# Where expert matrices are held and how the expert loop is cut, in a two-layer decoder step on one core

## What is computed

```python
scores = sigmoid(x @ w_router)                      # 16 experts, top 2 of the best group
combine = sum(one_hot(idx, 16) * w[..., None], 1)
h = silu(einsum('td,edf->tef', x, wg)) * einsum('td,edf->tef', x, wu)
h = h * combine[..., None]
out = einsum('tef,efd->td', h, wd)                  # then a layer norm
```

## Time and profile before

| | us |
|---|---|
| median of 3 runs | 1433.53 |
| lowest and highest | 1431.14 and 1434.43 |
| profiled execution, its own time | 1433.79 |
| its span in the trace | 1432.2 |
| PE busy with matmuls | 1220.3 (85%) |
| DVE, ACT, POOL busy | 463.7, 259.4, 155.9 |
| HBM read | 341.47 MB |

### The profile page before, as it was taken

One profiled execution on the slowest core, in us unless ns is written; L12 is line 12 of the kernel. 1 busy time (PEld: TensorE's weight loads), 2 busy tenths in 40 slices (PEclk: granted clock), 3 DMA queues, 4 the chain that ended last, 5 costly groups with the idle time before them and its releaser, 6 DMA issues.

```text
span 1432.2 us, 26802 instructions
## 1 busy us (share of the span) xinstructions
PE 1220.3 (85%) x10864; PEld 789.4 (55%) x10865; DVE 463.7 (32%) x1207; ACT 259.4 (18%) x540; POOL 155.9 (11%) x249
## 2 busy tenths in 40 slices
PE   6998788999989989868996997999897799858950
PEld 4686555667747745434453776767575355434420
DVE  0025637312422423312334005133315134313235
ACT  0005622211411301100102112023204111101101
POOL 2005991000000000000002000000000000000022
PEclk9999988999999989978998896999997799989885
DMA  9656789733684689999958131235747797999420
GB/s 330 221 147 207 225 269 386 260 117 118 236 323 174 238 360 392 430 424 429 413 202 291 66 125 56 69 111 190 281 173 287 290 369 305 430 424 426 167 78 35
DMA packets 89237, 360.64 MB, mean 252 GB/s; under 512 B 7111, under 2 KB 7127, under 8 KB 72762
## 3 DMA queue, kind: packets, MB, share of 16 engines
q1 hardware_dynamic: 80418, 331.50, 60.6%
q0 software_dynamic: 8592, 27.68, 5.6%
q10 hardware_dynamic: 144, 0.26, 0.1%
HBM read 341.47 MB, written 18.38 MB: 251 GB/s over the span
## 4 chain that ended last, share of the span: by engine, by line
PE 71%; DMA 11%; DVE 10%; issue 4%; ACT 2%; SPq 1%; POOL 0%; POOLq 0%; DVEq 0%; ACTq 0%
PE acc L710 42%; PE psS L710 14%; DMA ring<-in_w_exp_up 8%; PE psV L710 6%; DVE mixq L1433 2%; PE acc L1002 2%; PE acc L813 1%; PE psN L1106 1%; DMA ring<-in_w_in_even 1%; PE acc L1136 1%; DMA arena<-by_slot,arena 1%; DVE arena L1816 1%; PE psN L710 1%; DVE arena L1818 1%; DMA by_slot<-zT 1%
## 5 line engine op out<-in xcount | busy, mean ns | idle before, releaser
L710 PE MATMUL acc<-xT,ring 128*128 128x288 f32 x768 | 192.8, 415 | 4.1 <-DMA ring<-in_w_in_even 4.1
L710 PE MATMUL psS<-ring,zT 128*32 128x256 f32 x2368 | 150.4, 411 | 30.0 <-DMA ring<-in_w_exp_up 24.2
L710 PEld LDWEIGHTS acc<-xT,ring 128*128 128x128 f32 x768 | 149.1, 195 | 47.2 <-issue 5.3
L710 PEld LDWEIGHTS psS<-ring,zT 128*32 128x32 f32 x2368 | 78.0, 118 | 101.5 <-issue 36.2
L710 PE MATMUL acc<-mixq,ring 128*128 128x288 f32 x512 | 127.7, 413 | 2.7 <-DVE mixq L1666 1.6
L1791 DVE COPY zT<-psV 32x256 f32<-32x256 f32 x208 | 87.0, 418 | 115.0 <-DMA by_slot<-zT 79.3
L710 PEld LDWEIGHTS acc<-mixq,ring 128*128 128x128 f32 x512 | 98.7, 193 | 31.1 <-DVE mixq L1666 2.0
L710 PE MATMUL acc<-arena,zT 128*32 128x256 f32 (+1 forms) x1296 | 98.0, 411 | 11.9 <-issue 8.4
L1308 ACT ACTIVATE arena<-acc 128x1024 f32<-128x1024 f32 (+7 forms) x98 | 72.1, 758 | 109.9 <-PE acc L710 34.5
L1782 DVE TENSOR_TENSOR zT<-zT,psS 64x256 f32<-64x256 f32 x52 | 22.1, 424 | 211.9 <-ACT zT L2047 211.9
L2166 POOL DMA_DIRECT2D by_slot<-zT x52 | 25.6, 492 | 546.8 <-DVE zT L1791 546.8
(11 more groups left out here) (331 smaller groups left out, 1369.0 us busy)
## 6 DMA issues: line engine op xcount, KB each, us to landing
ring<-in_w_exp_gate SPq DMA_DIRECT2D x22, 2048.0 KB, 14.0
ring<-in_w_exp_up SPq DMA_DIRECT2D x22, 2048.0 KB, 18.5
ring<-in_w_exp_down SPq DMA_DIRECT2D x22, 2048.0 KB, 18.1
mixq<-in_w_exp_down SPq DMA_DIRECT2D x10, 2048.0 KB, 11.2
arena<-in_w_exp_gate SPq DMA_DIRECT2D x10, 2048.0 KB, 12.6
arena<-in_w_exp_up SPq DMA_DIRECT2D x10, 2048.0 KB, 17.3
ring<-in_cache_k SPq DMA_DIRECT2D x64, 256.0 KB, 3.1
ring<-in_cache_v SPq DMA_DIRECT2D x64, 256.0 KB, 3.0
```

What stands on the lines that cost most here:

```text
L710: return pe.matmul(out, lhsT, rhs, start=first, stop=last)
```

## The change

Eleven places instead of nine can hold expert matrices. xT, rs and std now lie in one buffer with mixq and zT; a place WIDE covers the rest of qT, xT, rs and std, and is free once x has been transposed (`xtok`, tile 5). A place ARENA_D covers 2 MiB of the arena in the odd layer only. The even layer fills ten places in its first pass and the odd layer eleven; after that both cycle through nine, so from expert 4 on the wait is still for expert e - 3 (`matrix_done(..., NE * l + 2 + 3 * i + j // 3)`).

PE writes expert 0 out and runs experts 1 to 15 in a loop of five rounds of three. The last round skips the work for a following expert by `pe.If(i < last)`. `turn_h` moves from the end of one expert to behind the register loads of the next. At the head the order is fetch(0), turn_x(0), gate_and_up(0), fetch(1), turn_x(1), then the tile of memory keys (even layer), then expert 0. DVE's `pick(2)` moves behind `hidden(0)`. ACT follows the same order. YS moves to partitions 32 to 63 of the arena. GAMMA and BETA are loaded after POOL's loop, behind the last store.

```diff
-SLOTS, EXTRA = 6, 3
+SLOTS, EXTRA, CYCLE = 6, 5, 9
...
-        YS = work[0:CAP, 896:1920]
+        YS = arena[32:32 + CAP, 2048:3072]
...
-        extra = [mixq.rearrange("p f m -> p (f m)")[:, 0:UNIT], view(3072, UNIT), view(3072 + UNIT, UNIT)]
+        extra = [acts[:, 0:UNIT], view(3072, UNIT), view(3072 + UNIT, UNIT), acts[:, UNIT:2 * UNIT],
+                 view(12800, UNIT)]
...
             if k[2] == 0:
-                around = [(at + j) % SLOTS for j in range(SLOTS)]
-                cycle = around[:5] + [SLOTS + j for j in range(EXTRA)] + around[5:]
-                at = around[3]
-            PLACE.append(cycle[k[2] % len(cycle)])
+                turn = [turn[(at + j) % SLOTS] for j in range(SLOTS)]
+                if k[1] + 1 < DEPTH:
+                    first = turn[:5] + [MIXQ, ARENA_B, ARENA_C, WIDE] + turn[5:]
+                else:
+                    first = turn + [MIXQ, ARENA_D, ARENA_B, ARENA_C, WIDE]
+            n = k[2]
+            while n >= len(first):
+                n -= CYCLE
+            PLACE.append(first[n])
...
-                            matrix_done(sp, j % 3, NE * l + j // 3 - 2 + 3 * i)
-                        e = 3 * i + j // 3
+                            e, at = 4 + 3 * i + j // 3, u + 12 + j
+                            matrix_done(sp, j % 3, NE * l + 2 + 3 * i + j // 3)
...
-                if l + 1 < DEPTH:
-                    memory_keys(l + 1, (1,))
-
                 for i in range(6):
                     evacuated(pe, f"xtok{l}", i)
...
                     extra = pe.value_load(STEPI[0:1, bass.ds(2 * n, 1)], min_val=0, max_val=NFURTHER)
                     first = pe.value_load(STEPI[0:1, bass.ds(2 * n + 1, 1)], min_val=0, max_val=NCHUNK - 1)
+                    turn_h(S, first)
                     expert_in(e, 2, i)
...
+                    if last is None:
+                        on()
                     else:
+                        with pe.If(i < last):
+                            on()
                         pe.wait_ge(S.rows, c + 2)
                     down(S, c, Wd)
                     mark(to_mark, down_used)
-                    if into is not None:
-                        turn_h(S, c + 1)
...
                 turn_x(S, 0, to_turn)
-                fetch(S, 1, to_split, True)
                 expert_in(0, 0, 0), expert_in(0, 1, 0)
                 gate_and_up(S, 0, Wg, Wu)
+                fetch(S, 1, to_split, True)
                 turn_x(S, 1, to_turn)
-                turn_h(S, 0)
+                if l + 1 < DEPTH:
+                    memory_keys(l + 1, (1,))
                 pe.wait_ge(steps_ready, l + 1)
-                with pe.Fori(0, NE // 3 - 1) as i:
-                    expert(0, 3 * i, i, i)
-                    expert(1, 3 * i + 1, i, i)
-                    expert(2, 3 * i + 2, i, i + 1)
-                for e in range(NE - 4, NE):
-                    expert(e, e, e // 3, (e + 1) // 3 if e + 1 < NE else None)
+                expert(0, 0, 0)
+                with pe.Fori(0, NE // 3) as i:
+                    expert(1, 3 * i + 1, i)
+                    expert(2, 3 * i + 2, i)
+                    expert(3, 3 * i + 3, i, NE // 3 - 1)
...
-                if l + 1 == DEPTH:
-                    pool.dma_start(GAMMA, ln_g[l, 2:3].to_broadcast([P, D])).then_inc(ln_rows, 16)
-                    pool.dma_start(BETA, ln_b[l, 2:3].to_broadcast([P, D])).then_inc(ln_rows, 16)
...
                     pool.dma_start(by_slot[slot_rows(c)], YS).then_inc(S.stored, 16)
+                if l + 1 == DEPTH:
+                    pool.wait_ge(gate_up_used, NE * l + 1)
+                    pool.dma_start(GAMMA, ln_g[l, 2:3].to_broadcast([P, D])).then_inc(ln_rows, 16)
+                    pool.dma_start(BETA, ln_b[l, 2:3].to_broadcast([P, D])).then_inc(ln_rows, 16)
                 pool.wait_ge(S.stored, 16 * last + 16)
```

83 lines of the change are left out of this document (45 added, 38 removed).

## The result

The changed kernel takes 1413.24 us (median of 4 executions, 1408.51 to 1416.25), the kernel before beside it 1432.34 (4 executions): a ratio of 0.9871, interval 0.9828 to 0.9915. Forecast were 1426.3 us in a range of 1416 to 1438, so the direction held and the size did not. Two later comparisons on other chips gave 0.9897 (0.9814 to 0.9980) and 0.9929 (0.9905 to 0.9954). The first comparison was a favourable draw; 12 us is what there is to explain, 7 were forecast.

The account below looks back on a forecast made before the run. PE's path to expert 4's or 5's mark, a fixed weight stream, and PE's path from expert 12's matrices set each stage; -8.5 - 1.9 - 2.4 + 2.5 + 2.3 + 0.8 = -7.2 us gave 1426.3 us, range 1416 to 1438.

Parts of the forecast that it names:

- odd head: Odd layer's first experts: earlier first mark, but new code waits at experts 0, 1 and 3; +2.5 us, bounds -3 and +7.
- odd tail: Odd layer's expert 13: idle time by issue goes, fetch and gate and up at full speed; -8.5 us, between -7 and -9.5.
- even head: Even layer's start: first mark +2.6 us later, less slow clock at experts 0 and 1; -2.4 us, bounds +2 and -4.2.
- even tail: Even layer's last experts: idle times of 1.06 and 1.10 us go; -1.9 us, -1 to -2.2.
- register work: turn_h's wait from a loaded register at 21 experts, loop's If in five: +2.3 us, bounds 0 and 3.5.
- end: Kernel's end: GAMMA and BETA loads ahead of the six gathers in POOL's queue; +0.8 us, bounds 0 and 3.
- three written-out experts shorter (about 1565): Code up to the odd head, setting packet boundaries 76, 60 and 30 instructions behind jumps of experts 0, 1 and 3.
- price list: Odd head: jump to packet 3.7 or 6.3 us, less 2.3, 1.9, 0.9 before the boundary: waits 1.0, 3.1, 4.7 us.
- signs of being wrong: First-round waits of 6 us each, q8 packets in rounds 2 to 5, or no wait at expert 12's matrices.
- my bound of the rival: First-round jumps each wait 6.2 us, then run slow by 3.3: +17.5 at worst, +7.5 likelier, 1434; chance 0.20.
- The places: More matrix places cost at nothing, bounds 0 to -5 us a layer; rival that they help, 1421, chance 0.10.
- third part's stream: Stages' weight loads from expert 4 on: not moved by more places, each load still waiting for the same mark; 0 us.

Follow-up runs that it names:

- before_pad_28: Kernel before with 28 one-column matmuls (112 instructions) in front of the odd layer's router, nothing else changed: 1410.66 us; repeated as 28b, 1411.37 us.
- before_2: Kernel before, unchanged, run once more for a second trace: 1428.29 us, ratio 1.0007.
- pad_odd_17: Changed kernel with 17 one-column matmuls (68 instructions) in front of the odd layer's router: 1422.07 us, ratio 0.9950.
- old_head: Changed kernel with the old head order on PE and ACT (memory keys ahead of gathers, fetch(1) ahead of gate and up): 1406.09 us; repeated as old_head_2, 1408.30 us.
- loop_alone: Kernel before with only the recut loop (expert 0 written out, five rounds of three); nine places, old head order, old turn_h: 1414.75 us.
- pad_odd_27: Changed kernel with 27 one-column matmuls (108 instructions) before the odd layer's router, loop ending at 1813: 1433.95 us (1416.2 to 1463.5).
- pad_odd_54: Changed kernel with 54 one-column matmuls (216 instructions) before the odd layer's router: 1411.80 us, ratio 0.9884.
- old_head_pad_54: Changed kernel with the old head order and 54 one-column matmuls before the odd layer's router, none in the even layer: 1404.21 us, ratio 0.9833.
- pad_odd_21: Changed kernel with 21 one-column matmuls (84 instructions) before the odd layer's router, loop ending at 1789: 1422.88 us (1416.7 to 1429.8).
- pad_odd_23: Changed kernel with 23 one-column matmuls (92 instructions) before the odd layer's router, loop ending at 1797: 1434.71 us (1417.2 to 1447.7).

## Why the prediction was right or wrong

Each step beside what the traces give: two of the kernel before (four for the even layer, whose code before_pad_28 shares), three of the changed kernel.

| step | forecast, us | measured, us |
|---|---|---|
| odd head, to expert 4's first mark | +2.5 | -4.1 (102.2 to 98.1) |
| odd stream, expert 4 to 12 | 0 | +0.7 |
| odd tail, expert 12 to 15 | -8.5 | -8.4 (64.8 to 56.5) |
| even head, to expert 4's first mark | -2.4 | +0.1 (96.5 to 96.6) |
| even stream, expert 4 to 12 | 0 | -0.7 |
| even tail | -1.9 | -1.3 |
| register work, spread over the above | +2.3 | none of its own visible |
| end, behind expert 15's first mark | +0.8 | +0.9 (55.4 to 56.3) |
| sum | -7.2 | -12.8 |

The sum of -12.8 stands beside the 12.4 us of the three comparisons. The first comparison alone had 18.4; the rest of it lies outside these stages, and the 3.5 us between them are chance, as before_2 shows.

**The step that failed: the odd head.** It is 6.6 us off, more than the 5.6 us by which the sum is off. The mechanism held: a wait is the time from jump to packet less what PE does before the boundary. pad_odd_17, which puts the boundaries where I had them, came out 3.7 us above the kernel before at expert 4's mark (105.9 against 102.2) for a forecast of 2.5, and at 7.7 for 7.2 in time. What was wrong is the number under it, "three written-out experts shorter (about 1565)", by 185 instructions: 76, 60 and 30 should have been 147, 129 and 96. In its place the runs showed waits of 0, 2.15 and 2.61 us for the 1.0, 3.1 and 4.7 forecast, and a head of -4.1 us for +2.5.

The price list itself was only about right, and its working doesn't come out. From 3.7 us (expert 0) and 6.3 us (experts 1 and 3) to the packet, less 2.3, 1.9 and 0.9, the waits would be 1.4, 4.4 and 5.4 us, and the odd head +4.9 and not +2.5. pad_odd_17 has 0.71, 3.71 and 3.95. None of the signs of being wrong that I had named came: the first-round waits stayed far below 6 us, q8 was empty, and the waits at expert 12's matrices were there. No sign tested the count of places, which was the step that failed.

My range doesn't follow from my bounds either. They add up to 21.7 us below and 14.7 above the forecast, and two thirds of that are 14.5 and 9.8, so 1412 to 1436: not the -16 and +6 that I wrote, and not 1416 to 1438.

**The odd tail** was right in size (-8.4 for -8.5), and half right in cause. I read the 5.80 us as the price of code behind the loop. before_pad_28b keeps that code, its packets too, and loses 5.4 us of them, though 1.92 come back 62 matmuls on; its tail is 6.7 us shorter in all. What the kernel before paid was mostly a jump 17 instructions behind a boundary. Nor was my bound of the rival, that every first-round jump waits 6.2 us, near: the changed kernel's waits are 2.15 and 2.61.

**The even head** is 2.5 us worse than forecast, and by chance looked better in the first pair of traces. The 3.24 us of idle time are as forecast, and the first mark came at 503.40 for 505.7 forecast (1.3 us of this because the stage began sooner). But the 503.05 of the earlier trace rows to which I compared was a slow draw, 32.5 us behind the router: the four traces that share this code have 32.5, 30.2, 32.5 and 30.3. Old order with the rest of the change has it at 28.3. The order costs 6.3 us there, and I had valued its return, the 3.3 and 1.7 us of slow clock, as its own gain. I don't know which other part of the change gives that return: old_head differs from loop_alone (28.3 against 29.8 us, and 9.3 against 11.9 for expert 0) in the places, in `turn_h`'s place behind the register loads and in `pick(2)`, and these were not tried one by one.

**Register work**, +2.3 in the forecast, has no trace of its own in any stage, and 0.1 us in each of 26 places would have been 2.6. After the odd head it is the largest part of the miss towards faster.

**The places** were not worth nothing: 3 to 4 us in the even layer, 5.6 to 6.4 us in time. The false sentence is that the third part's stream begins at expert 4 in the even layer. I showed that it has no gap from there and took this for its beginning. In the kernel before, the DMA engines bring 388 GB/s from 503 to 569 us, with fortieths of this window at 139 to 238; in the changed kernel they bring 418 GB/s from 503 to 655 us, and after the first fortieth of this window no fortieth falls below 390. That is 29 matrices without a gap from expert 0's first mark. The bound that I gave, one matrix or 4.96 us, was nearer than my value. In the odd layer, where experts 1 to 5 hold PE longer, they give nothing, as forecast (277.6 and 276.7 with nine, 277.1 to 277.5 with eleven): there the transfers nearly run dry between 1194 and 1202 us in the changed kernel (DMA share 0.20), and the stream does begin behind that, at expert 5's first mark.

**The end** has the right size by another cause. The last `down` took 3.46 us in place of 1.93, PE being near the 1.2 GHz level there (granted clock 0.55); from its mark to the span's end it is 51.3 us in all three traces of the changed kernel, 51.6 and 51.7 with nine places and the early rows. GAMMA and BETA in front of the gathers cost nothing.

The Trainium skill, "Runtime: NRT & Kernel Launch", section "Instruction fetch mechanics", gives TensorE a store of 2048 instructions in blocks of 256, and a few lines on a window of two pages outside which a jump must fetch. The runs agree with the blocks of 256 (one boundary in 256 instructions fits every stall in the last table of this document), and do not contradict the 2048: a loop within seven blocks stays, one that reaches into an eighth need not. That the eighth block of the store holds what is fetched ahead would fit, but no run shows it. The runs disagree with the window of two pages, as the earlier trace rows did.

## What to carry to other kernels

Where a profile shows idle time by issue near a jump, first move the code, by padding that hides beside a wait, before crediting or blaming an edit: here 112 useless instructions were worth as much as the whole change, and a change that alters the length of code ahead of a loop carries such a gain or loss with it. Compare parts in place-neutral pairs, as the head's order here, which cost 8 us inside a change that won 12. And when a stream of transfers has no gap from some mark on, look for its real first gap further back before costing anything ahead of that mark at nothing.

## What the runs showed of the hardware that I had not expected

The wait at or behind a jump over 255 instructions, in the odd layer, against the distance of the jump from the packet boundaries (same count as above; expert, kernel). More than one value means more than one trace. The kernels with nine places, whose code lies one instruction off, have 1.0 to 1.5 us at or behind expert 1's jump and 2.2 to 2.6 behind expert 3's:

| jump, instructions past the last boundary | boundary, ahead | wait, us |
|---|---|---|
| 12 (3, pad_odd_27) | 244 | 5.60, at the jump |
| 17 (13, before and before_2) | 239 | 5.80, 6.11, at the jump |
| 87 (1, before_pad_28 and 28b) | 169 | 2.05, 2.40, at the jump |
| 87 (1, pad_odd_54 and old_head_pad_54) | 169 | 1.02, 1.28, behind it |
| 127 (1, changed) | 129 | 2.15 in all three, behind it |
| 129 (13, before_pad_28 and 28b) | 127 | 1.83, 1.92, behind it |
| 160 (3, changed) | 96 | 2.61, 2.63, 2.05, behind it |
| 160 (3, old_head and old_head_2) | 96 | 3.17, 0.71, behind it |
| 195 (1, pad_odd_17) | 61 | 3.71, behind it |
| 211 (1, pad_odd_21) | 45 | 4.19, behind it |
| 219 (1, pad_odd_23) | 37 | 4.70, behind it |
| 228 (3, pad_odd_17) | 28 | 3.95, behind it |
| 231 (1, before and before_2) | 25 | 4.61, 3.81, behind it |
| 235 (1, pad_odd_27) | 21 | 4.92, behind it |
| 244 (3, pad_odd_21) | 12 | 5.03, behind it |
| 252 (3, pad_odd_23) | 4 | 5.18, behind it |

In these runs a jump of experts 1, 3 or 13 close on either side of a boundary cost 3.8 to 6.1 us, and one in the middle 0.7 to 3.2. A gather right behind such a wait took 2.94 us and not 1.64 (expert 3, pad_odd_21 and 23). I read it so: just past a boundary the next packet has only been asked for, and the jump itself waits for it; just before one, the packet after the target is missing. The traces show where PE waits, not what was asked for when.

Expert 0 is cheaper at the same distance: 0.71, 0.89, 1.39 and 1.88 us at 79, 63, 55 and 39 ahead of a boundary (pad_odd_17, 21, 23, 27). Its 1.88 us stand beside expert 1's 4.70 at 37 ahead. From the mark to the end of the wait the DMA share was 0.02 for the one and 0.98 for the other. Expert 0 of the kernel before, 42 ahead, waits 0.77 and 0.47 us. That the transfers of weights delay the packet is the likely reason; it was not tried by itself.

And a loop that doesn't quite fit is not a constant loss but a lottery: from 1417 to 1448 us with 23 pads, and in the one trace that shows it (27 pads) one round fetched again, not all.
